# Gated linear attention in pairs of chunks: one state update for 128 tokens instead of two for 64

## The reference, cut to what matters

```python
bcum = jnp.cumsum(heads(gk, GLA_HK), axis=-2)           # within a chunk of 64
q_t = qf * jnp.exp(bcum)
k_t = kf * jnp.exp(-bcum)
attn = jnp.where(causal, einsum('nbhik,nbhjk->nbhij', q_t, k_t), 0.0)
o_intra = einsum('nbhij,nbhjv->nbhiv', attn, vf)
k_dec = kf * jnp.exp(b_last - bcum)
def step(S, xs):
    q_c, k_c, v_c, bl = xs
    o = einsum('bhik,bhkv->bhiv', q_c, S)
    S = S * jnp.exp(bl)[..., 0, :, None] + einsum('bhjk,bhjv->bhkv', k_c, v_c)
    return S, o
```

## Time and profile before

| | us |
|---|---|
| median of 3 runs (lowest, highest) | 2009.32 (2008.55, 2010.96) |
| span of the profiled execution, first to last instruction | 2005.4 |
| TensorE busy | 1958.8 |
| VectorE busy | 1338.7 |
| ScalarE busy | 839.2 |

### The profile page before, as it was taken

One profiled execution on the slowest core, in us unless ns is written; L12 is line 12 of the kernel. 1 busy time (PEld: TensorE's weight loads), 2 busy tenths in 40 slices (PEclk: granted clock), 3 DMA queues, 4 the chain that ended last, 5 costly groups with the idle time before them and its releaser, 6 DMA issues.

```text
span 2005.4 us, 33165 instructions
## 1 busy us (share of the span) xinstructions
PE 1958.8 (98%) x14158; PEld 1669.7 (83%) x14158; DVE 1338.7 (67%) x1761; ACT 839.2 (42%) x1262; POOL 117.2 (6%) x123
## 2 busy tenths in 40 slices
PE   8999899999999999999999999999999999999998
PEld 6877777777889989887989888989987678889887
DVE  5476667566578767767546587776666757767765
ACT  4334634244344434444323353443444645434432
POOL 1154000000000000010000000000002200000000
PEclk9999999999999999999999999999999999999999
DMA  8222214035413323324230132333332112323331
GB/s 262 85 70 83 83 34 136 24 107 87 103 63 104 99 92 105 106 65 126 85 103 24 43 106 85 105 105 100 98 135 79 54 42 84 106 85 105 105 99 49
DMA packets 138546, 182.13 MB, mean 91 GB/s; under 512 B 4805, under 2 KB 103253, under 8 KB 138016
## 3 DMA queue, kind: packets, MB, share of 16 engines
q1 hardware_dynamic: 135392, 168.91, 26.0%
q0 software_dynamic: 3008, 11.11, 2.7%
HBM read 172.66 MB, written 7.34 MB: 90 GB/s over the span
## 4 chain that ended last, share of the span: by engine, by line
PE 91%; DVE 5%; ACT 2%; issue 1%; DMA 1%; SPq 0%; DVEq 0%; ACTq 0%
PE X L1475 19%; PE M L1387 18%; PE M L1388 18%; PE M L1389 18%; PE X L641 2%; PE M L1448 1%; PE M L1450 1%; PE M L1449 1%; PE M L641 1%; PE M L1799 1%; PE X L1787 1%; DVE w_lo L2259 1%; PE X L1776 1%; PE X L1387 1%; PE X L1388 1%
## 5 line engine op out<-in xcount | busy, mean ns | idle before, releaser
L1388 PE MATMUL M<-u,raw_lo 128*128 128x512 f32 x728 | 287.9, 396 | 0.0
L1387 PE MATMUL M<-u,w_hi 128*128 128x512 f32 x728 | 287.9, 395 | 0.0
L1389 PE MATMUL M<-u,w_hi 128*128 128x512 f32 x728 | 286.1, 393 | 0.0
L1881 ACT ACTIVATE w_hi<-raw 128x2048 fp32r<-128x2048 f32 (+1 forms) x114 | 215.8, 1893 | 87.9 <-PE M L1450 42.9
L1936 ACT ACTIVATE us<-X 128x256 f32<-128x256 f32 x156 | 60.0, 385 | 427.2 <-PE X L1475 427.2
L2404 DVE TENSOR_TENSOR h<-h,M 128x512 f32<-128x512 f32 x184 | 123.5, 684 | 145.1 <-PE M L1389 144.9
L1475 PE MATMUL X<-t,w_hi 128*128 128x256 f32 x936 | 173.2, 282 | 0.0
L1389 PEld LDWEIGHTS M<-u,w_hi 128*128 128x128 f32 x728 | 137.7, 189 | 32.9
L1387 PEld LDWEIGHTS M<-u,w_hi 128*128 128x128 f32 x728 | 136.8, 188 | 30.8
L1388 PEld LDWEIGHTS M<-u,raw_lo 128*128 128x128 f32 x728 | 136.7, 188 | 29.8
L2259 DVE TENSOR_TENSOR w_lo<-raw,w_hi 128x2048 fp32r<-128x2048 f32 (+1 forms) x57 | 129.4, 2270 | 34.5 <-ACT w_hi L1881 34.5
(11 more groups left out here) (550 smaller groups left out, 4617.9 us busy)
## 6 DMA issues: line engine op xcount, KB each, us to landing
raw<-in_w_up_dram SPq DMA_DIRECT2D x48, 1024.0 KB, 5.4
raw<-in_w_down_dram SPq DMA_DIRECT2D x48, 1024.0 KB, 5.1
raw<-in_w_in_dram SPq DMA_DIRECT2D x12, 1024.0 KB, 8.2
raw<-in_a_w_in_dram SPq DMA_DIRECT2D x12, 1024.0 KB, 5.4
h<-in_x_dram SPq DMA_DIRECT2D x16, 256.0 KB, 7.6
raw<-in_w_mk_dram SPq DMA_DIRECT2D x4, 1024.0 KB, 5.3
raw<-in_w_mv_dram SPq DMA_DIRECT2D x4, 1024.0 KB, 5.2
raw<-in_w_out_dram SPq DMA_DIRECT2D x4, 1024.0 KB, 6.8
```

The costliest lines, as they stand in the source:

```text
L1387: mm(dst, wh, xh, start=start, stop=False)
L1388: mm(dst, wl, xh, start=False, stop=False)
L1389: return mm(dst, wh, xl, start=False, stop=stop)
L1881: nc.scalar.activation(hi_of(n)[:, :, 0:cols], raw[:, n % 4, :, 0:cols], ACT.Copy).then_inc(S["w_hi_ready"], 1)
```

## The change

- The recurrence steps by 128 tokens: one state per pair. `inter` is called once per pair, for 128 columns, and not for the first; `state_products` once for each of the first three pairs, with 128 rows. `state_bank` is X[2], X[3] alone.
- What crossed the border between a pair's two chunks through the state is now in the scores: 4 extra products of `gk` (even chunk, 64 columns of weights) with `gq` (odd chunk, 64 columns) into the upper right block of X[0], and `gla` lets the whole triangle through.
- `pair_adjust` (VectorE), after the scores of a pair: multiplies the odd chunk's `gq` by the even chunk's exp(b_last) and the even chunk's `gk` by the odd chunk's, in place; for pair 0, the decays of pairs 1 and 2 (`g_elp`) in one small product instead of the first of these.
- The transposes are a step of their own, `pair_keys`, which waits for `pair_adjust`, and are gone for the last pair. Pair 0's stand between the two last chunks of the gate's projection.
- VectorE does `pair_result` ahead of the mask, ScalarE does `keys_out` after the squares, and several waits are other ones.

```diff
--- before.py
+++ after.py
@@ -74,7 +74,7 @@
     put("low32", (a // 32 == b // 32) & (a // 16 > b // 16))
     put("low64", a // 32 > b // 32)
     put("eye64", a == b)
-    put("gla", (p // 64 == f // 64) & (p <= f))
+    put("gla", p <= f)
     put("sel0", p == f % 64)
     put("sel1", p == 64 + f % 64)
     put("plusminus", np.where(p == 0, 1.0, np.where(p == 1, -1.0, 0.0)))
@@ -421,7 +421,7 @@
         ma_small = [[small[:, 64 + 16 * j + 4 * i:68 + 16 * j + 4 * i] for i in range(4)] for j in range(2)]
         sinkb = small[:, 32:48]
         sw_small = [[small[:, 48 + 40 * j + 8 * i:56 + 40 * j + 8 * i] for i in range(5)] for j in range(2)]
-        g_el = small[:, 64:96]
+        g_el, g_elp = small[:, 64:96], small[:, 104:112]
         fold_w = small[:, 16:24]
         gain_neg = small[:, 112:120]
         fold_c = [small[:, 96 + 4 * i:100 + 4 * i] for i in range(2)]
@@ -939,22 +939,30 @@
             def pair_scores(cp):
 
                 tok = slice(cp * P, cp * P + P)
+                even, odd = slice(cp * P, cp * P + 64), slice(cp * P + 64, cp * P + P)
                 if cp:
                     wait("g_at", cp)
                 for hd in range(4):
-                    last = mm(X[0][:, hd * P:hd * P + P], gb[:, hd, tok], gq[:, hd, tok], start=True, stop=True)
+                    mm(X[0][:, hd * P:hd * P + P], gb[:, hd, tok], gq[:, hd, tok], start=True, stop=True)
+                for hd in range(4):
+                    last = mm(X[0][0:64, hd * P + 64:hd * P + P], gk[:, hd, even], gq[:, hd, odd], start=True, stop=True)
                 last.then_inc(S["g_kt"], 1)
+
+            def pair_keys(cp):
+
+                tok = slice(cp * P, cp * P + P)
+                wait("g_sc", 24 + 2 * cp + 2)
+                if cp:
+                    wait("g_ktev", cp)
                 if cp >= 2:
                     wait("g_rl", cp - 1)
-                if cp:
-                    wait("g_ktev", cp)
                 for hd in range(4):
                     last = nc.tensor.transpose(X[1][:, hd * P:hd * P + P], gk[:, hd, tok], C("ident"))
                 last.then_inc(S["g_kt"], 1)
 
             def pair_norm(cp):
                 wait("g_sq", 2 * (cp + 1))
-                wait("g_ktev", min(cp + 2, 4))
+                wait("g_ktev", min(cp + 2, 3))
                 for hd in range(4):
                     for vc in range(2):
                         a_ = (2 * (hd % 2) + vc) * P
@@ -965,55 +973,58 @@
                 return [M[2 * (cp % 2)], M[2 * (cp % 2) + 1]]
 
             def intra(cp):
-                if cp:
-                    wait("g_s", 2 * cp)
+                if cp < 2:
+                    wait("acc_evac", ACC[N_GG] + 6 + 2 * cp)
                 else:
-                    wait("acc_evac", ACC[N_GG] + 6)
+                    wait("g_oev", 4 * (cp - 2) + 2)
                 wait("g_at", cp + 1)
-                wait("g_ktev", cp + 1)
                 for hd in range(4):
                     for vc in range(2):
                         a_ = (2 * (hd % 2) + vc) * P
-                        mm(out_banks(cp)[hd // 2][:, a_:a_ + P], gv[:, cp, hd * 256 + vc * P:hd * 256 + vc * P + P],
-                           gat[cp % 2][:, hd, :], start=hd % 2 == 0 and vc == 0, stop=False, skip_group_check=True)
-
-            def inter(c):
-                wait("g_s", c)
+                        last = mm(out_banks(cp)[hd // 2][:, a_:a_ + P], gv[:, cp, hd * 256 + vc * P:hd * 256 + vc * P + P],
+                                  gat[cp % 2][:, hd, :], start=hd % 2 == 0 and vc == 0, stop=cp == 0, skip_group_check=True)
+                if cp == 0:
+                    last.then_inc(S["g_o"], 1)
+
+            def inter(cp):
+                wait("g_s", cp)
+                wait("g_sc", 24 + 2 * cp + 1)
+                tok = slice(cp * P, cp * P + P)
                 for hd in range(4):
                     for vc in range(2):
-                        a_ = (2 * (hd % 2) + vc) * P + 64 * (c % 2)
-                        last = mm(out_banks(c // 2)[hd // 2][:, a_:a_ + 64], gs[c % 2][:, hd, vc * P:vc * P + P],
-                                  gq[:, hd, 64 * c:64 * c + 64], start=False, stop=c % 2 == 1, skip_group_check=True)
-                if c % 2:
-                    last.then_inc(S["g_o"], 1)
+                        a_ = (2 * (hd % 2) + vc) * P
+                        last = mm(out_banks(cp)[hd // 2][:, a_:a_ + P], gs[cp % 2][:, hd, vc * P:vc * P + P],
+                                  gq[:, hd, tok], start=False, stop=True, skip_group_check=True)
+                last.then_inc(S["g_o"], 1)
 
             def state_products(cp):
+                wait("g_ktev", cp + 1)
                 if cp:
-                    wait("g_oev", 4 * (cp - 1) + 2)
-                else:
-                    wait("acc_evac", ACC[N_GOUT])
+                    wait("g_s", cp)
                 for hd in range(4):
-                    for c2 in range(2 if cp < 3 else 1):
-                        r = slice(64 * c2, 64 * c2 + 64)
-                        last = mm(state_bank(2 * cp + c2, hd), gkt[cp % 2][r, hd, :], gv[r, cp, hd * 256:hd * 256 + 256],
-                                  start=True, stop=True)
+                    last = mm(state_bank(hd), gkt[cp % 2][:, hd, :], gv[:, cp, hd * 256:hd * 256 + 256], start=True, stop=True)
                 last.then_inc(S["g_n"], 1)
 
             pair_scores(0)
             chunk(N_GG + 3, 0, g_hi, g_lo_)
+            pair_keys(0)
             chunk(N_GG + 3, 1, g_hi, g_lo_)
             for cp in range(4):
                 intra(cp)
                 if cp:
-                    inter(2 * cp)
-                state_products(cp)
-                if cp:
                     pair_norm(cp - 1)
                 if cp < 3:
                     pair_scores(cp + 1)
-                inter(2 * cp + 1)
+                if cp:
+                    inter(cp)
+                if cp < 3:
+                    state_products(cp)
+                if cp < 2:
+                    pair_keys(cp + 1)
             wait("g_lo", 4)
             for j in range(4):
+                if j == 0:
+                    wait("g_oev", 10)
                 if j == 2:
                     wait("g_oev", 14)
                 chunk_tokens(N_GOUT + j // 2, j % 2, g_hi, g_lo_, 0, 256, False)
@@ -1024,10 +1035,9 @@
                 chunk_tokens(N_GOUT + j // 2, j % 2, g_hi, g_lo_, 256, T, True)
             blocks(N_GOUT + 2, 2, g_hi, g_lo_)
 
-        def state_bank(c, hd):
-
-            t = X[2 + hd // 2] if c % 2 == 0 else M[2 * ((c // 2 + 1) % 2) + hd // 2]
-            return t[:, (hd % 2) * 256:(hd % 2) * 256 + 256]
+        def state_bank(hd):
+
+            return X[2 + hd // 2][:, (hd % 2) * 256:(hd % 2) * 256 + 256]
 
         def cs(c):
 
@@ -1095,9 +1105,6 @@
             for cp in range(4):
                 if cp:
                     pair_norm(cp - 1)
-                if cp < 3:
-                    keys_out(cp + 1)
-                if cp:
                     pair_hi(cp - 1)
                 if cp == 1:
                     hi(N_GOUT + 1)
@@ -1108,6 +1115,8 @@
                     act.wait_ge(S["g_gate"], KT)
                 for i in range(2):
                     nc.scalar.activation(nt[i][:], M[2 * (cp % 2) + i][:], ACT.Square).then_inc(S["g_sq"], 1)
+                if cp < 2:
+                    keys_out(cp + 1)
             pair_norm(3)
             pair_hi(3)
 
@@ -1158,10 +1167,24 @@
                 nc.vector.copy_predicated(gat[cp % 2][:], C("gla").bitcast(i32).unsqueeze(1).to_broadcast([P, 4, P]),
                                           X[0][:].rearrange("p (h n) -> p h n", h=4)).then_inc(S["g_at"], 1)
 
+            def pair_adjust(cp):
+
+                dve.wait_ge(S["g_kt"], 2 * cp + 1)
+                el = g_el.rearrange("p (h c) -> p h c", h=4)
+                if cp == 0:
+                    TTO(g_elp.rearrange("p (h c) -> p h c", h=4), el[:, :, 2:6:2], el[:, :, 3:7:2], ALU.mult).then_inc(S["g_sc"], 1)
+                else:
+                    odd = gq[:, :, cp * P + 64:cp * P + P]
+                    TTO(odd, odd, el[:, :, 2 * cp:2 * cp + 1].to_broadcast([P, 4, 64]), ALU.mult).then_inc(S["g_sc"], 1)
+                if cp < 3:
+                    even = gk[:, :, cp * P:cp * P + 64]
+                    TTO(even, even, el[:, :, 2 * cp + 1:2 * cp + 2].to_broadcast([P, 4, 64]), ALU.mult).then_inc(S["g_sc"], 1)
+
             for b in range(4):
                 lo(N_GG + b + 1)
                 if b == 3:
                     pair_mask(0)
+                    pair_adjust(0)
                 for c in range(2):
                     k = 2 * b + c
                     evac(N_GG + b, c, gg[:, k, :])
@@ -1169,18 +1192,19 @@
                     STT(gg[:, k, :], gg[:, k, :], V("a_onorm_2", c), nt[c][:], ALU.mult,
                         ALU.mult).then_inc(S["g_gate"], 1)
 
-            def state(c):
-
-                dve.wait_ge(S["g_n"], c // 2 + 1)
-                if c:
```

(22 more changed lines are left out.)

## The result

The change makes the kernel faster: 1994.7 us (median of 5 runs, 1993.7 to 1999.6) against 2008.6 for before on the same chip (median of 5, 2006.9 to 2011.0), a ratio of 0.9936, 95% interval 0.9918 to 0.9954. The forecast was 2000.8 with a range from 1998.7 to 2005.0: the direction was right, the gain was 13.9 us where 8.5 were forecast, and the time lies under the range. The profiled execution of after spans 1992.9 us, 12.5 less than that of before.

A forecast was written before the change was run, and what follows sets the result against it. TensorE, busy for 98% of the span, was taken as the bound. 7.16 + 1.92 + 0.3 + 0.39 + 1.9 - 3.2 = 8.5 us off 2009.3 gave 2000.8 us, range 1998.7 to 2005.0.

The forecast's parts named there:

- the fixed difference of 3.9 us: Whole kernel: the runs' median, 2009.3 us, stays 3.9 above the profiled span of 2005.4 after the change too.
- (a): `inter` on TensorE: 7 calls of 64 tokens become 3 of 128 at the same cost per call; 7.16 us less.
- (b): State products on TensorE: 3 calls instead of 4, 1.92 us less; the three that stay gain 0.3 in all.
- (c): Transposes of the last pair's keys on TensorE go: 0.39 us less.
- (d): TensorE's three waits in the stage go: 1.9 us less, if nothing else is late.
- (e): Four added groups of off-diagonal products on TensorE: 0.8 us each, 3.2 us more, ends 2.4 and 5.0.
- (f): VectorE has about 4 us less work, ScalarE one `keys_out` fewer; neither is on the path, so nothing is booked.
- (g): First pair's transposes, behind a gate chunk, wait for VectorE's first scaling: cover 0.5 us at least, cost nothing.
- The two covers: Slack before TensorE waits: 1.0 us for VectorE's scalings before pair 2's transposes, 0.7 for `keys_out(2)` before pair 1's norm.
- R1: Rival: both covers fail and a new wait takes part of the gain; 2.5 us back gives 2003.3; chance 0.07.
- R2: Rival: off-diagonal products eat the gain; at 2.9 us a group nothing is left, 2009.3 us; chance 0.07.
- R3: Rival: the granted clock falls to half in the stage after a late wait; slower, 2023.8 us; chance 0.03.

The follow-up runs named there:

- e7: After with two more multiplications into dead buffers on VectorE, ahead of the scalings of pair 2: stage 42.71 us.
- e8: After with four more multiplications into dead buffers on VectorE, ahead of the scalings of pair 2: stage 43.92 us.
- e3: After without the four groups of off-diagonal products, so some scores are wrong: stage 39.95 us.
- e4: An edit of after; the text doesn't tie the label to one: `inter` in halves (stage 47.79 us), `inter` of 64 columns (42.46) or 64-row state products (43.31).
- e9: After with decays summed over 128 tokens, a pair as one chunk, no off-diagonal products or scalings: 1993.4 us, ratio to before 0.9927, stage 39.59 us.
- e1: The kernel before, unchanged, run once more: ratio to before 1.0011; its profiled execution spans 2016.0 us.

## Why the prediction was right or wrong

The mechanism of the change was right: fewer instructions of TensorE, three waits gone, none in their place. The time missed by 6.1 us, in three parts: 2.1 from the base, 2.9 from the clock, 1.1 from the sum. The steps that failed are the fixed difference of 3.9 us and the clock's share, put at nothing but 1 us at each end of the range.

**The base.** "the median of the runs, 2009.3, is 3.9 above it, and I take that difference as fixed". This step failed. In all runs with a recorded span, the time is 1.8 to 1.9 us above the span of the same execution. The profiled execution of before had therefore taken about 2007.2 (an estimate), and the median of three runs was 2.1 us above it, most likely because those runs had more of the stretches at half clock (their clocks aren't recorded, so this isn't shown).

**The clock.** The sum was made from one execution's rows, and the range had 1 us at each end for the runs. This failed too. The 51 runs of before lie between 2001.7 and 2018.6 us and the 17 of after between 1991.6 and 2008.9, nearly all of it by the clock. I had read the 0.50 of the earlier trace rows as something that a late wait may cause in the stage, and didn't ask how much of it the execution held elsewhere, nor whether it would come again. Had I done so, the range would have been several microseconds wider. That the measured gain was 13.9 us is then luck of the clock too: by the lines above, the two medians stand for 11.7 and 7.7 us lost to the clock (an estimate), and at equal clock the gain is 9.6 to 10.1 us. In the longer series it is 8.4 by the ratio and 9.3 by the medians.

**The sum, term by term.**
(a) right: 4 x 1.79, confirmed by two experiments.
(b) right in kind, too small: the slots gave 2.82 us where 2.22 were booked. They fell from 1.92 to 1.62, three times 0.3 where I took 0.1 and allowed 0.2. And I missed that entering the mode of 64 rows is paid in the slot ahead. Two calls of `inter` before a state product took 1.94 in before, not 1.79 (1087.27 to 1089.21 is one), and the first `intra` 2.11, against 1.90 in after: 0.5 us in all. I read the pause behind (0.33) and not the one ahead.
(c) wrong: nothing was gained. One group of transposes went, but the three that stay became dearer, 0.55 for 0.39. They now follow directly on products that move 256 or 512 columns; where a wait stands between (e7, e8) they take 0.39 again.
(d) right: all three waits went, and none came. Start to start they were worth 2.1 us, not 1.9.
(e) right: 2.95 us for the four groups in the table, 3.2 by e3, where I took 3.2, though for a reason that I had half. 0.61 a group are its own, and 0.1 to 0.2 stand ahead.
(f), (g) right: nothing of VectorE or ScalarE is late. The cover of (g), put at 0.5 us at least, is 0.32 in after (the scaling ends at 1048.48, the transposes begin at 1048.80), as e3 shows too: with the products gone, the transposes wait 0.58.
So 8.5 became 9.6 by 0.6 in the slots of (b), 0.5 at the entries, 0.2 in (d) and 0.25 in (e), less 0.4 in (c).

Outside the stage, less half of the half-clock stretches, all profiles of kernels with the beginning unchanged have 1944.1 to 1945.3 us of span, but e4 1947.4 and e9 1946.8. The excess lies ahead of the decay products (L931): reckoned the same way, e4 takes 922.4 us up to there and e9 921.2, the others 919.3 to 920.5. No edit of e4 or e9 touches that part, so I take it for a difference between executions; what it is stays open.

**What is late next.** The two covers were put at 1.0 and 0.7 us. The first is 0.84 in the trace (scalings end at 1068.44, transposes begin at 1069.28), and e7 and e8 agree. The second is 0.53 in the trace of after, from the end of the copy to the norm at 1071.61:

```profile
1068.02 0.42 DVE L1181 TENSOR_TENSOR gk<-gk,small 128x256 f32<-128x256 f32 x1
...
1070.48 0.60 ACT L1049 ACTIVATE gkt<-X 128x512 f32<-128x512 f32 x1
```

Counted from the norm before (1062.39), ScalarE's chain took 8.69 us, as forecast (8.7); TensorE took 9.22 and not 9.5. In e3 the chain is as long (8.70), but TensorE comes there after 8.4, and so the norm waits.

**The rule.** Three groups put back into the mode of 64 rows cost 0.87 us, and a pause of 0.2 stands ahead of each off-diagonal group. By the Trainium skill, TensorEngine Tiling (Array Packing), section Key Properties, a change of mode drains the TensorE. The runs agree that such changes cost time; that a drain is what they show isn't tested. I had counted eight changes that go against eight that come, and put the time by the rule at 1999.3: in the direction of the truth, but by a wrong price, since a group cost 0.7 to 0.8 and not 0.42.

**Rivals.** R1: no wait came. R2: 0.8, not 2.9. R3: the clock in the stage stayed at 1.00. It fell elsewhere, and in both kernels.

## What to carry to other kernels

When a float32 product's weights are 128x128 and it moves 64 to 128 columns, count instructions: halving their number by doubling the columns gave the full half (7.2 us here), and the slots, start to start, gave it before the change was built. Where groups with 64 rows or 64 columns of weights stand between full ones, look for their price on both sides: the entry stands in the slot of the group ahead, the exit in the pause before the group behind. And before a small gain is forecast in absolute time, take the spread of the runs with their mean clocks, and compare spans at equal clock: the stage repeated to 0.01 us while whole runs of one kernel differed by 17.

## What the runs showed of the hardware that I had not expected

- TensorE was at 1.2 GHz for 3.4 to 20.5 us at a time, with its busy time the whole stretch (20.50 of 20.50 us at 0.50 in e1). Which places have it changes from one execution to the next, though some recur: near 316 us in ten of thirteen profiles. Only the one near 927 us could be tied to what ran before it.
- Half of the rows in the mode of 64 took longer than all 128 without it: 1.92 against 1.62 us for the same 8 instructions.
- A stretch at 0.50 followed four sixteen-row products in a row in eleven of eleven profiles. Spread among full ones they kept the clock at 1.00, and 4.5 us of pauses for eight instructions, against 2.6 in a row, took most of it back.
